# Two layers written out with constant waits, and the modulation sums begun later in each layer

## The reference

```
cond = silu(c)
for l in 0, 1:
    shift, scale, gate = split(cond @ w_mod[l] + b_mod[l])      # 3 x 1024
    h = rmsnorm(x, norm_g[l]) * (1 + scale) + shift
    P = h @ w_in[l]
    y_a = hgrn2(P: q, f, i) * silu(P: g)          # 4 heads
    y_b = mla(P: c_q, c_kv, k_rope) * silu(P: g)  # 8 heads, causal softmax
    y_c = retention(P: q, k, v) * silu(P: g)      # 4 heads
    m = sum over b of sigmoid(P: merge_b) * (y_b @ w_p,b)
    x = x + gate * (m @ w_out[l])
return rmsnorm(x, final_g)
```

## Time and profile before

| | us |
|---|---|
| median of 3 runs | 1443.9 (1442.6 to 1444.5) |
| the profiled execution | 1443.96 |
| its span, first to last instruction | 1442.2 |
| PE busy | 1323.3 (92%) |
| DVE busy | 758.0 (53%) |
| ACT busy | 641.3 (44%) |
| POOL busy | 601.4 (42%) |

### The profile page before, as it was taken

The page is one execution under the profiler, slowest core; times in us unless marked ns, Lnnn a source line. Parts: engine busy times, 40 slices in busy tenths (PEclk is TensorE's granted clock), DMA queues, the critical chain, the costliest instruction groups (busy, mean ns, idle before and its releaser), DMA issues.

```text
span 1442.2 us, 20431 instructions
## 1 busy us (share of the span) xinstructions
PE 1323.3 (92%) x5886; PEld 1040.6 (72%) x5886; DVE 758.0 (53%) x1174; ACT 641.3 (44%) x988; POOL 601.4 (42%) x756
## 2 busy tenths in 40 slices
PE   0389889999999999999978988999999999999996
PEld 0177677888777777778856777778877777778884
DVE  6877876533455424433337787653346541444333
ACT  2245544544455334444334555455445533444531
POOL 3243333464323444545534332346432344445451
PEclk9999999999999999999988999999999999999998
DMA  9132212244223233333323222224422223333331
GB/s 368 38 102 74 70 55 89 83 136 125 79 72 94 86 106 106 88 105 110 89 76 109 72 61 61 92 83 133 131 74 74 84 99 98 104 91 111 101 97 59
DMA packets 46057, 140.06 MB, mean 97 GB/s; under 512 B 5744, under 2 KB 5744, under 8 KB 45680
## 3 DMA queue, kind: packets, MB, share of 16 engines
q1 hardware_dynamic: 28656, 102.65, 23.6%
q10 hardware_dynamic: 17280, 35.99, 7.8%
HBM read 136.52 MB, written 2.10 MB: 96 GB/s over the span
## 4 chain that ended last, share of the span: by engine, by line
PE 78%; DVE 12%; issue 4%; ACT 4%; DMA 1%; ACTq 1%; DVEq 0%
PE ps_st L663 21%; PE ps_st L665 21%; PE ps_st L664 21%; PE ps_o L685 4%; PE ps_s L755 2%; PE ps_s L710 2%; PE ps_s L779 1%; PE ps_w L764 1%; DVE pro_acc L1131 1%; PE ps_misc L680 1%; DMA pro_w<-w_mod_first 1%; DVE hg_x L1340 1%; DVE h_lo L1400 1%; DVE gate_x L1190 1%; PE ps_misc L671 1%
## 5 line engine op out<-in xcount | busy, mean ns | idle before, releaser
L576 POOL TENSOR_TENSOR w_lo<-raw,w_hi 128x256 fp32r<-128x256 f32 x744 | 588.3, 822 | 793.9 <-ACT w_hi L839 793.5
L663 PE MATMUL ps_st<-h_hi,w_hi 128*128 128x512 f32 x1008 | 416.5, 413 | 0.7 <-POOL w_lo L576 0.4
L665 PE MATMUL ps_st<-h_hi,w_lo 128*128 128x512 f32 x1008 | 398.6, 395 | 0.0
L664 PE MATMUL ps_st<-h_lo,w_hi 128*128 128x512 f32 x1008 | 398.2, 395 | 0.0
L663 PEld LDWEIGHTS ps_st<-h_hi,w_hi 128*128 128x128 f32 x1008 | 193.3, 192 | 48.9 <-issue 8.3
L664 PEld LDWEIGHTS ps_st<-h_lo,w_hi 128*128 128x128 f32 x1008 | 192.7, 191 | 44.6 <-issue 6.2
L665 PEld LDWEIGHTS ps_st<-h_hi,w_lo 128*128 128x128 f32 x1008 | 192.1, 191 | 41.8
L839 ACT ACTIVATE w_hi<-raw 128x1024 fp32r<-128x1024 f32 x186 | 195.2, 1050 | 29.9 <-PE ps_st L665 27.5
L861 ACT ACTIVATE gate_t<-gate_x 128x512 f32<-128x512 f32 x80 | 50.6, 632 | 242.2 <-DVE gate_x L1190 242.2
L1190 DVE TENSOR_SCALAR gate_x<-ps_st 128x512 f32<-128x512 f32 x80 | 55.2, 690 | 193.0 <-PE ps_st L665 191.4
L710 PE MATMUL ps_s<-hg_x 128*128 128x128 f32 x384 | 54.4, 292 | 28.7 <-DVE hg_x L1340 28.7
(11 more groups left out here) (233 smaller groups left out, 1987.9 us busy)
## 6 DMA issues: line engine op xcount, KB each, us to landing
raw<-w_stream SPq DMA_DIRECT2D x186, 512.0 KB, 3.6
mod_w<-w_mod ACTq DMA_DIRECT2D x96, 256.0 KB, 2.7
pro_w<-w_mod_first ACTq DMA_DIRECT2D x16, 512.0 KB, 12.7
x<-x_t SPq DMA_DIRECT2D x4, 512.0 KB, 10.5
ret_decay<-decay ACTq DMA_DIRECT2D x2, 1024.0 KB, 4.9
out_t<-o_t SPq DMA_DIRECT2D x8, 256.0 KB, 2.2
cs<-cst SPq DMA_DIRECT2D x1, 906.5 KB, 5.2
pos_i<-positions ACTq DMA_DIRECT2D x1, 256.0 KB, 7.3
```

Of the source, the lines that this page charges most:

```text
L576: ins = nc.gpsimd.tensor_tensor(w_lo[:, i % RING, r], raw[:, i % RING, r], w_hi[:, i % RING, r].bitcast(F32), ALU.subtract)
L663: nc.tensor.matmul(dst[0:m, :], wh, hi, start=(k == 0), stop=False)
L664: nc.tensor.matmul(dst[0:m, :], wh, lo, start=False, stop=False)
L665: last = nc.tensor.matmul(dst[0:m, :], wl, hi, start=False, stop=(k == nk - 1))
```

## The change

The two layers are written out: the body of the loop is built twice, layer is a Python number, and each wait compares with a constant. With it go the registers, the additions for the waits and for the addresses of transfers, and the branch at the end of a layer. And add_mod_steps leaves the first 22 items of a layer without modulation steps; all 54 steps are spread over the 59 items after them, from item ckv 0 to item pc 1. The last step stands where it stood.

```diff
@@ add_mod_steps
-    total = N_ITEMS - 12
+    first = ITEM_AT[("ckv", 0)]
+    total = N_ITEMS - 12 - first
     for s in SCHEDULE:
         out.append(s)
         if s[0] == "item":
             n += 1
-            while steps and len(steps) > (total - n) * (MOD_SECTIONS * (DT + 1)) / total:
+            if n <= first:
+                continue
+            while steps and len(steps) > (total - (n - first)) * (MOD_SECTIONS * (DT + 1)) / total:
                 out.append(steps.pop(0))
@@ class Counter
-    def __init__(self, eng, layer, per_layer):
-        self.eng, self.layer, self.per_layer = eng, layer, per_layer
+    def __init__(self, layer, per_layer):
+        self.layer, self.per_layer = layer, per_layer
         self.asked, self.own = {}, {}
-        self.base, self.value = {}, eng.alloc_register(name="wait_value")
-
     def at(self, sem, k):
         self.asked[id(sem)] = max(k, self.asked.get(id(sem), 0))
-        n = self.per_layer[id(sem)]
-        if n not in self.base:
-            self.base[n] = self.eng.alloc_register(name=f"layer_times_{n}")
-            self.eng.reg_mul(self.base[n], self.layer, n)
-        self.eng.reg_add(self.value, self.base[n], k)
-        return self.value
+        return self.layer * self.per_layer[id(sem)] + k
@@ on each of the five engines (here DVE)
-            with dve.Fori(0, DEPTH) as layer:
-                e = Counter(dve, layer, per_layer)
+            for layer in range(DEPTH):
+                e = Counter(layer, per_layer)
```

More of the change, by code:

```diff
@@ L540, in _ @@
                 sp.dma_start(x[:, j:j + 2, :], x_t[:, j:j + 2, :]).then_inc(x_in, 16)
-            with sp.Fori(0, DEPTH) as layer:
-                e = Counter(sp, layer, per_layer)
+            for layer in range(DEPTH):
+                e = Counter(layer, per_layer)
                 for i, it in enumerate(ITEMS):
@@ L567, in _ @@
                 pool.wait_ge(pro_sum, j + 1)
-            with pool.Fori(0, DEPTH) as layer:
-                e = Counter(pool, layer, per_layer)
+            for layer in range(DEPTH):
+                e = Counter(layer, per_layer)
                 for i, it in enumerate(ITEMS):
@@ L591, in _ @@
             last.then_inc(pro_mod_sum, 1)
-            with pe.Fori(0, DEPTH) as layer:
-                e = Counter(pe, layer, per_layer)
+            for layer in range(DEPTH):
+                e = Counter(layer, per_layer)
                 def take(key):
@@ L823, in _ @@
             act.preload_act_table_set(TABLE_SET)
-            with act.Fori(0, DEPTH) as layer:
-                e = Counter(act, layer, per_layer)
+            for layer in range(DEPTH):
+                e = Counter(layer, per_layer)
                 gated = []
```

## The result

The changed kernel took 1431.7 us (median of four, 1429.8 to 1432.6) against 1444.1 us: a ratio of 0.9919, 95% interval 0.9906 to 0.9932. The forecast was 1428.7. The change gives 12.4 us where 15.2 were forecast; the largest miss among the terms is what the moved steps cost where they went, 5.4 us instead of 1.8.

A forecast was written before the change was run, and what follows sets the result against it. PE, busy for 92% of the span, was taken to bound the kernel, losing time in the HGRN2 parts. -11.2 - 3.4 - 0.7 - 1.7 + 1.8 = -15.2 on 1443.96 gave 1428.7 us, range 1418 to 1439.

The forecast's parts named there:

- The waits: HGRN2 parts: modulation steps gone shorten PE's seven numbered waits a layer (third, fourth -0.9 each, fifth -0.3, seventh -1.1); -11.2 us.
- near 2.1: Sign in the HGRN2 part: PE's first wait, 4.22 us before, falls to about this many us.
- near nothing: Sign in the HGRN2 part: PE's seventh wait, 1.25 us before, all but goes, a gain of 1.1 us.
- The clock: HGRN2 parts: PE loses 19.3 us in all at the lower clock; two falls fewer were taken, -3.4 us.
- rival A: HGRN2 parts: with shorter waits most clock falls go, 12.9 us instead of 3.4, 1419 us; chance 0.18.
- PE's handovers: Some five late handovers a layer on PE have a second wait, which constants make cheaper: 10 x 0.07, -0.7 us.
- Rival D: Extra waits and the edge between layers cost what they did despite the constants; 1432.5 us; chance 0.08.
- The edge: Between the layers: without the loop's branch rstd begins earlier, then held by PE's column sum; -1.7 us.
- within 2.5: Sign at the edge between layers: rstd starts at most this many us after the last square.
- The moved steps: Behind the HGRN2 part: second and third mod_sum hold PE before transposes in bank w1, four times 0.45 us; +1.8 us.
- B: HGRN2 third, fourth, seventh waits: ACT's split and exponential hold instead of DVE, no clock fall goes; 1438 us; chance 0.20.
- C: MLA: a modulation step's transfer has not landed and holds DVE's queue at 16 mla_pt handovers; slower, 1464 us; chance 0.05.

The follow-up runs named there:

- e9: The change, with eight mod_acc of a layer put back behind later HGRN2 items (heads 1 to 3 and the last quarter); 1438.4 us, ratio 0.9967.
- e7: The change, with the first four mod_acc of a layer put back behind items 0, 1, 3 and 4; 1438.1 us, ratio 0.9961.
- e8: The change itself, run once more unaltered; 1431.8 us, ratio 0.9920 of the kernel before.
- e11: Repeat of e1: the changed kernel with the modulation steps in their old places; 1440.1 us, ratio 0.9976.
- e10: Repeat of e2: the kernel before, loop and registers kept, with only the new placing of the modulation steps; 1435.0 us, ratio 0.9943.
- e4: The change itself, run once more unaltered; 1432.3 us, ratio 0.9930 of the kernel before.
- e1: The changed kernel (constants, layers written out) with the modulation steps in their old places; 1438.1 us, ratio 0.9966.
- e5: The change, with the 54 steps laid out so that the second mod_sum stands behind bg 0, the third behind rk 0; 1427.9 us, ratio 0.9890.
- e6: As e5, but the steps begin three items later, behind ma 0, past the two norms; 1426.2 us, ratio 0.9882.
- e2: The kernel before, loop and registers kept, with only the new placing of the modulation steps; 1432.6 us, ratio 0.9931.
- e3: The kernel before with the two layers written out, but each wait still adding in a register, steps in their old places; 1441.5 us, ratio 0.9991.

## Why the prediction was right, and where it was not

**The waits (-11.2 forecast).** As a price of the steps the wait-by-wait working held: 6.4 for the third, fourth, fifth and seventh, and 6.3 measured by e9; 4.2 for the first, and by e7's and e8's traces hg_x comes 2.1 us later in each layer, 4.2 in all. e7 as a whole costs 6.3: 1.1 more is the longer window at half clock in layer 1, and the 1.0 left over is within the scatter (the two profiled executions lie 5.5 apart). Waits and clock together had 14.6: from e11 to e8, which differ by the move alone, the HGRN2 parts lose 17.7 us, 14.5 without the PE time of the four sums that left them (0.81 each); from the kernel before to e10, the move without the constants, it is 13.9 in the same way. What failed is the picture that the waits themselves would shrink by that. The old ones in layer 0 are shorter by 5.2 us (4.22 to 2.41, 2.15 to 1.89, 2.70 twice to 2.07 with their small companions, the fifth from 1.21 to 0.31, the seventh not at all), and two new ones of 1.99 have come. Of the signs named beforehand, "near 2.1" for the first wait was met by 2.41 at best (3.0 in e4 and e8), and "near nothing" for the seventh wasn't (1.37). A wait on an engine that paces the stage isn't a measure of what goes: when DVE's chain gets shorter, PE's clock rises as well, and PE waits for the same chain.

**The clock (-3.4 forecast).** The step that failed: "PE loses half of each" window, 19.3 us in all, as if each half were to be had. PE does lose it, but part or all of it is taken out of later waits, by where the fall stands: 1.6 us stay of one at 97 us, 0.9 of one behind a wait for hg_kd, nothing of e8's other three (from e4 to e8 layer 0's part differs by 0.05 us at most), where the forecast had one price of 1.7 to 2.1 for each. Nearly all the clock came back in the profiled execution (the mean of the HGRN2 parts is 1.00 and 0.99). So rival A's sign was there and its price wasn't: it gave 1419. No run has the clock by itself, so that waits and clock together came near 14.6 doesn't bear out the 3.4; the forecast had most falls remain, and most went.

**PE's handovers (-0.7) and the constants.** In the HGRN2 parts e8 is 1.3 and 1.5 us shorter than e10, and e11 0.9 and 1.4 shorter than the kernel before; e1's 0.9 and -0.5 show how far such a difference moves with the falls. With 2.3 at the edge the sum is near the forecast's (0.7, 1.7 and some 1.5 within the waits), but the single gap that the term was read from doesn't bear it out. It had 0.11 us between hg_q and the next operation. Ahead of hg_q the chain of the kernel before, then that of the changed one, read

```profile
87.98 0.64 ACT gate_t L876
88.62 0.02 issue
88.64 0.70 DVE hg_q L1202
```

```profile
88.63 0.03 issue
88.66 0.02 DVEq L1197
88.68 0.05 issue
88.73 0.70 DVE hg_q L1198
89.44 0.02 issue
89.46 1.24 DVE hg_b L1274
```

So an extra wait on a constant leaves an instruction of 0.02 us (L1197), where the addition took 0.04 (`DVEq L363` in the earlier trace rows). The gap behind hg_q has shrunk, but the one ahead of it has grown from 0.02 to 0.10. In e11, where the mod_acc still stands behind hg_q, the three gaps of this place are 0.10, 0.03 and 0.03 us, where they were 0.02, 0.11 and 0.12: 0.09 less in all. And up to the first hg_x the constants gave nothing: it comes 31.3 us after PE's first matmul in e1 and e11, and 30.8 in the kernel before. The Trainium skill (Perfetto Trace Analysis, "Identifying Dependency Chains"), weighed in the forecast, says that an instruction waiting on several engines may get a semaphore instruction ahead of it; this trace agrees, and its row (0.02 us) has the price. Rival D has fallen by the edge and by what the constants gave as a whole (e1 and e11, 3.7 us); where within the HGRN2 parts they gave it isn't shown.

**The edge (-1.7 forecast).** -2.3 in e8, and in e5, e6, e7 alike; the 2.65 us of issue are gone. The forecast took rstd to be held by the column sum, and that is what holds it now; it took the sum at its old 1.65 us, and in e8 it runs in 1.12, the 0.5 us that the term was short of. In the profiled execution and in e4 only 1.4 came. The rows of the change, then of e8 (a window, then the column sum), show why:

```profile
736.00:738.00 2.00, 0.00 (x0) 0.00 (x0) 1.18 (x2) 1.38 (x2) 0.00 (x0) 0.75 0.00 0
...
738.10 2.08 PE L676 MATMUL ps_misc<-sq_sum,cs 128*128 128x512 f32 x2 [3.15 <-DVE sq_sum L1279]
```

```profile
739.00:741.00 2.00, 1.12 (x2) 0.30 (x2) 0.20 (x1) 1.88 (x3) 1.57 (x3) 1.00 0.00 0
...
739.26 1.12 PE L676 MATMUL ps_misc<-sq_sum,cs 128*128 128x512 f32 x2 [3.16 <-DVE sq_sum L1279]
```

In the first the clock had fallen before the column sum, in the second behind it. So rstd starts 2.0 us behind the last square in e8 and 3.0 in the profiled change, where "within 2.5" was the sign. Here too a part is taken back: from the first matmul of the column sum to the end of layer 1's HGRN2 part are 217.0 us in e4 and in e8, and 217.7 in the profiled change.

**The moved steps (+1.8 forecast).** The clash in bank w1 was sized well: 0.56 and 0.54 us a layer, 2.2 in all. Two costs of the same move were missed, 1.8 for the sum that had covered the first mla_t's wait and 1.4 for POOL's w_lo behind the norms, where it is argued, and not followed in the trace, that DVE's first steps delay the norm, ACT's split and so POOL. The prediction had gone through the places to which steps come, not those which they leave, and took "DVE has time" from a mean over 230 us. 1.8 + 1.4 + 0.4 is 3.6 us too little, 0.6 more than the 3.0 by which the forecast missed; e5 and e6 gave 3.9 and 1.7 of it back.

**Rivals B and C.** For B, ACT stands in the chains as it said, and the seventh wait kept its size; but the steps gave their full price in time, so it has fallen. C's mechanism is there without its price: mod_acc does wait for its transfer, from the table of DVE's waits, 290 to 1432 us:

```profile
DVE mod_acc L1534 <- DMA mod_w<-w_mod: 19.2, 6, 4.3
```

Four of the six are of some 4.2 us, above the 1.45 from which it was to decide, and the kernel before has none; yet no wait of PE for mla_pt is in the table above, so they don't fall on the sixteen handovers. In e5 and e6 such waits remain (18.5 and 20.5 us in all), although both are faster than the change.

**Still open.** Why the same kernel's clock falls at 97 us in one execution and not in another, why a fall behind a wait for hg_kd costs and one behind a later wait for hg_x doesn't, and why e2's executions lie 2 us below e10's.

## What to carry to other kernels

Before a busy engine's wait or its low clock is booked as a gain, ask what paces the stage: if the releaser's chain does, price the change by what it takes out of that chain, and expect waits and clock to rearrange themselves, in part at no gain. Price lost clock by the place of the fall, from two executions that differ in it, and not by half its length. When steps move, look at what they covered where they stood, not only at what they collide with where they go. And a wait-by-wait sum can be tested cheaply by putting a few of the steps back.

## What the hardware showed beyond that

- The chain's pace is very even: from head 1 on, the starts of PE's matmuls in layer 0's HGRN2 part differ between e4 and the profiled change by a constant to within 0.05 us. In e8 they do so too, but for the stretches behind its three half-clock windows, where PE is up to 1.6 us later until its next wait.
- A loop's back edge cost this program 2.65 us of ACT's time, and without it the way between the layers is 1.6 us shorter in e3's trace (7.66 to 6.04); written-out code had no gap there, and the instruction transfers got smaller, not larger: one queue moved 0.29 MB instead of 0.57 in the whole run, with 16609 instructions instead of 20431.
- The two matmuls of the column sum took 2.08 us at a granted clock of 0.50 and 1.12 at 1.00.
